# Decode attention: query parts made once and copied by ScalarE, the weights scaled on GpSimd, the first score sum behind page 5

## The chip, the cores and the metric

The kernel runs on 1 core of one Trainium2 chip. The metric is the device time of one execution in microseconds (us). The engines are named as in the profile: PE is TensorE (PEld its weight loads), DVE is VectorE, ACT is ScalarE, POOL is GpSimd, SP the sync engine that issues the DMAs. L12 is line 12 of the kernel.

## The reference, cut to what matters

One step of a two-layer decoder: an mLSTM layer and a differential-attention layer, over a prompt of 1024 tokens and over 8 sample sequences of 4 new tokens each. The change lies in the attention of the sample sequences, which read 1024 cached positions each (8 pages of 128, through a page table):

```python
def diff_mix(q, k_parts, v_parts, masks, lam):
    scores = []
    for kp, mk in zip(k_parts, masks):
        s = jnp.einsum('bqhcd,bkhcd->bhcqk', q, kp) * ATTN_SCALE
        ...
    p = jax.nn.softmax(jnp.concatenate(scores, axis=-1), axis=-1)
    w = p[:, :, 0] - lam * p[:, :, 1]
    for vp in v_parts:
        o = jnp.einsum('bhqk,bkhe->bqhe', w[..., start:start + s_len], vp)
        ...
```

There are 8 heads, two query and key parts of 64 per head, 4 queries per sequence: 64 rows of scores per sequence, each 1056 wide (1024 cached and 32 new positions). All is fp32.

## The kernel before, in words

The kernel works in phases (norm, gates, mLSTM, output projection, attention of the prompt, decode, second output projection), separated in time. The change is in `decode_phase` (L2102 to L2489). Matmuls there take each fp32 number as a high and a low part: ACT copies the data into a high part (type fp32r), DVE or POOL subtracts that from the data to get the low part, and PE multiplies both.

**Per sequence b** the decode does this. T0 to T7 (`turn`, L2418): PE transposes the eight heads of a key page in two halves of four heads, into one of three PSUM banks in turn; K0 to K7: ACT (`k_high`, L2257) copies each half into XH, DVE (`k_low`, L2336) subtracts into XL and thereby frees the bank. A half-turn has to wait for the DVE step three half-turns earlier. S0 to S3 (`score`, L2432): 16 matmuls each against two key pages, QZ holding the queries (high parts in 64 columns, low parts in the next 64). R0 to R2: ACT copies the lower 64 rows of a score bank (L2272), DVE adds the two (L2349). M: DVE adds the mask (L2355), takes the row maximum (L2356) and scales it (L2357). E: ACT takes the exponential of all 1056 columns with its sum (L2284); DVE takes the reciprocal (L2369), multiplies by a sign and lambda (L2370, giving `cf`, 64x1) and scales the 64x1056 weights with it (L2371). W: PE transposes the weights (L2452), DVE sums the two parts (L2376, L2378), ACT makes the high part (L2290, L2291), DVE the low part (L2384, L2386, both inputs in SBUF). V0 to V7 (`value`, L2457): for each value page ACT makes the high part (L2267), POOL the low part (L2240), and PE does four matmuls; then the new tokens' values (N, L2472), and ACT copies the output out (O, L2297). Q: before the keys of a sequence, ACT copies its queries' high parts from QS into QZ (L2280, two instructions) and DVE subtracts to get the low parts (L2364, two instructions with both inputs in SBUF).

**Order.** Every engine walks through a body b = 0 to 9 in an order written out by hand. In body b the keys of sequence b are turned and scored, the weights of sequence b-1 are made and its value pages 0 to 3 multiplied, and value pages 4 to 7 of sequence b-2 are finished. Bodies 2 to 7 are a hardware loop; 0 and 1 and the last two stand outside it. Body 0 has only keys, bodies 8 and 9 only weights and values.

```python
PE_ORDER = ("T0", "V4", "V5", "T1", "V6", "T2", "V7", "N", "T3", "S0", "W", "S1",
            "T4", "V0", "T5", "V1", "T6", "V2", "T7", "S2", "V3", "S3")
ACT_ORDER = ("Q", "K0", "V0", "E", "K1", "V1", "K2", "V2", "K3", "V3", "O", "W",
             "K4", "V4", "K5", "R0", "V5", "K6", "V6", "K7", "R1", "V7", "R2")
DVE_ORDER = ("Q", "K0", "K1", "E", "K2", "K3", "W", "K4", "R0", "K5", "K6", "K7", "R1", "R2", "M")
```

POOL has only the value pages' low parts, in order of pages, each behind ACT's high part. PE's V0 waits for the low weights (`wlo`, L2461), its W for the scaled weights (`wd`, L2448).

**Loads.** Key pages and value pages (512 KB each) have four slots each. SP issues them alternately, the next key page when PE has turned the page four before, the next value page when POOL has finished the page four before, all in one queue in order.

Of the kernel before, what the change touches and what calls it, by code (L numbers as in the profile page):

```python
# [17 lines left out]
ALU = mybir.AluOpType  # L18
ACT = mybir.ActivationFunctionType
F32 = mybir.dt.float32  # L20
F32R = mybir.dt.float32r
# [3 lines left out]
P = 128  # L25
D = 1024
# [77 lines left out]
def trunk_step(  # L104
# [20 lines left out]
    def phase_tensor(name, shape, dt=F32):  # L125

        return scratch[-1].enter_context(nc.sbuf_tensor(name, shape, dt))
# [27 lines left out]
    with ctx:  # L155
# [1944 lines left out]


        def decode_phase():  # L2102
            take = area(AREA - 3 * P * NT // 2 - 3 * TS)
            G = 2 * P
            NEW = PAGES * P
            ROWS = H * 2 * DS
# [1 line left out]
            VB = take(4, D)  # L2108
            SR, SX = take(TOK), take(TOK)
            AVS = take(D)  # L2110
            QS = take(H, TS)
            WS = take(NB * TS)
            sgn, mx, nm, sm, rc, cf = (take(1) for _ in range(6))
            QZ = WH[:, 0:H * 136]
            WTS = WH[:, 1088:1088 + NB * 64].rearrange("p (a c) -> p a c", a=NB)

            VH2 = phase_tensor("VH2", [P, 2, D], F32R)
            VH = [WH[:, 1664 + s * D:1664 + (s + 1) * D] for s in range(2)] + [VH2[:, s, :] for s in range(2)]
            VL = [WL[:, s * D:(s + 1) * D] for s in (0, 1, 3, 4)]
# [1 line left out]
            d_in, d_avs, d_yr = sem("d_in"), sem("d_avs"), sem("d_yr")  # L2121
            k_ld = [sem(f"d_k{s}") for s in range(4)]
            v_ld = [sem(f"d_v{s}") for s in range(4)]
            ini, pre, pre2, tp, kh, kl, sc, slo, add, mxs, exd, wd, wtp, wr, whi, wlo, vh, vl, av, avd, avc, qh, ql, vn = (
                sem(f"d_{s}") for s in ("ini", "pre", "pre2", "tp", "kh", "kl", "sc", "slo", "add", "mx", "ex", "w", "wtp",
                                        "wr", "whi", "wlo", "vh", "vl", "av", "avd", "avc", "qh", "ql", "vn"))
            dch = sem("d_dve")

            S_AT = [(BK[2], 0, G), (BK[2], G, G), (BK[3], 0, G), (BK[6], 0, G + TS)]
# [7 lines left out]

            PE_ORDER = ("T0", "V4", "V5", "T1", "V6", "T2", "V7", "N", "T3", "S0", "W", "S1",
                        "T4", "V0", "T5", "V1", "T6", "V2", "T7", "S2", "V3", "S3")
            ACT_ORDER = ("Q", "K0", "V0", "E", "K1", "V1", "K2", "V2", "K3", "V3", "O", "W",  # L2140
                         "K4", "V4", "K5", "R0", "V5", "K6", "V6", "K7", "R1", "V7", "R2")
            DVE_ORDER = ("Q", "K0", "K1", "E", "K2", "K3", "W", "K4", "R0", "K5", "K6", "K7", "R1", "R2", "M")

            def sequences(eng, body, links=None, per=0):

# [11 lines left out]
            def has_keys(b):  # L2157

                return not isinstance(b, int) or b < DB
# [17 lines left out]
            with nc.Block() as block:  # L2177
# [57 lines left out]
                @block.gpsimd  # L2235
                def _(pool):
                    with pool.Fori(0, DB) as i:
                        for p in range(PAGES):
                            pool.wait_ge(vh, PAGES * i + p + 1)
                            nc.gpsimd.tensor_tensor(VL[p % 4], VB[:, p % 4, :], VH[p % 4].bitcast(F32), ALU.subtract)\  # L2240
                              .then_inc(vl, 1)

                @block.scalar
                def _(act):
                    act.wait_ge(d_in, 48)
                    act.wait_ge(pre, 1)
                    act.activation(QS, BK[2][:, 0:H * TS].rearrange("p (h t) -> p h t", h=H), ACT.Copy)
                    act.activation(XH[:, :, NEW:TOK], BK[2][:, H * TS:2 * H * TS].rearrange("p (h t) -> p h t", h=H),
                                   ACT.Copy).then_inc(pre2, 1)
                    act.activation(VHN[0:TS, :], AVS[0:TS, :], ACT.Copy).then_inc(vn, 1)  # L2250
                    act.wait_ge(pre2, 1)
                    act.wait_ge(ini, 2)

                    def body(b):
                        i = b - 1
# [18 lines left out]
                        def queries():  # L2274

                            wait(act, sc, 4 * b)
                            for c in range(2):
                                rows = slice(DK * c, DK * c + DK)
                                dst = QZ.rearrange("p (h r) -> p h r", r=136)[rows, :, DS * c:DS * c + DS]
                                act.activation(dst, QS[rows, :, bass.ds(b * DS, DS)], ACT.Copy).then_inc(qh, 1)  # L2280

                        def exponentials():
                            act.wait_ge(mxs, i + 1)
# [34 lines left out]
                def _(dve):  # L2318
# [7 lines left out]
                    dve.wait_ge(ini, 2)  # L2326
                    dve.wait_ge(pre2, 1)
                    v.tensor_tensor(XL[:, :, NEW:TOK], BK[2][:, H * TS:2 * H * TS].rearrange("p (h t) -> p h t", h=H),
                                    XH[:, :, NEW:TOK].bitcast(F32), ALU.subtract).then_inc(vn, 1)
                    dve.wait_ge(vn, 2)  # L2330
                    v.tensor_tensor(VLN[0:TS, :], AVS[0:TS, :], VHN[0:TS, :].bitcast(F32), ALU.subtract).then_inc(vn, 1)

                    def body(b):
# [22 lines left out]
                            links.link(v.tensor_reduce(mx[0:64, :], SR[0:64, :], AX, ALU.max, negate=True))  # L2356
                            v.tensor_scalar(nm[0:64, :], mx[0:64, :], ATTN_SCALE, None, ALU.mult).then_inc(mxs, 1)  # L2357

                        def queries():
                            for c in range(2):  # L2360
                                rows = slice(DK * c, DK * c + DK)
                                z = QZ.rearrange("p (h r) -> p h r", r=136)[rows, :, :]
                                dve.wait_ge(qh, 2 * b + c + 1)
                                v.tensor_tensor(z[:, :, 64 + DS * c:64 + DS * c + DS], QS[rows, :, bass.ds(b * DS, DS)],  # L2364
                                                z[:, :, DS * c:DS * c + DS].bitcast(F32), ALU.subtract).then_inc(ql, 1)

                        def shares():
                            dve.wait_ge(exd, i + 1)
                            links.link(v.reciprocal(rc[0:64, :], sm[0:64, :]))  # L2369
                            links.link(v.tensor_tensor(cf[0:64, :], rc[0:64, :], sgn[0:64, :], ALU.mult))  # L2370
                            v.tensor_scalar(SR[0:64, :], SR[0:64, :], cf[0:64, :], None, ALU.mult).then_inc(wd, 1)  # L2371

                        def weights_low():

# [13 lines left out]

                        for step in DVE_ORDER:
                            if step[0] == "K" and has_keys(b):  # L2390
                                k_low(int(step[1]))
                            elif step[0] == "R" and has_keys(b):
                                add_rows(int(step[1]))
                            elif step == "M" and has_keys(b):
                                maximum()
                            elif step == "Q" and has_keys(b):
                                queries()
                            elif step == "E" and has_weights(b):
                                shares()
                            elif step == "W" and has_weights(b):  # L2400
                                weights_low()
                    sequences(dve, body, links, 4)

                @block.tensor
                def _(pe):
# [9 lines left out]
                    def body(b):  # L2415
# [16 lines left out]
                        def score(g):  # L2432
                            bank, at, n = S_AT[g]
                            pe.wait_ge(kl, 2 * PAGES * b + 4 * (g + 1))
                            if g == 0:
                                pe.wait_ge(ql, 2 * b + 2)

                            wait(pe, add, 3 * i + (1, 1, 2, 3)[g])
                            m = 0
                            for h in range(H):  # L2440
                                for k in (XH, XL):
                                    x = nc.tensor.matmul(bank[:, at:at + n], QZ[:, h * P:(h + 1) * P],
                                                         k[:, h, g * G:g * G + n], start=(m == 0), stop=(m == 2 * H - 1))
                                    m += 1
                            x.then_inc(sc, 1)
# [88 lines left out]
```

## Time and profile before

| what | value |
|---|---|
| median of 3 runs | 1851.96 us (1850.69 to 1852.35) |
| the profiled execution | 1853.36 us |
| its span, first to last instruction | 1851.6 us |
| decode, first body's keys to the last output | about 1449 to 1733 us of the span |
| busy share of the span | PE 91%, PEld 74%, DVE 55%, ACT 45%, POOL 23% |
| mean granted PE clock | 0.950 |
| DMA | 172 MB, mean 93 GB/s |

Times in the trace are from the start of the span. A line of a timeline has the start, the length, the engine, the source line, the operation, what it writes and reads, the count of merged instructions, and in brackets how long the engine stood idle before it and what ended that. The windows view gives the busy time of each engine in a stretch, and the clock granted to PE in it as a share of full speed.

### The profile page before, as it was taken

The numbers are of one execution on the slowest core, as the hardware profiler recorded it, in microseconds if no ns is written. First come the engines' busy times: TensorE is split into PE (matmuls) and PEld (weight loads), VectorE is DVE, ScalarE is ACT, GpSimd is POOL, SyncE is SP. The second block draws the span as 40 slices with busy tenths as digits, with TensorE's granted clock in tenths as the row PEclk, the third lists the DMA queues.
The fourth block names the chain that finished last, engine by engine and source line by source line (L and its number), as shares of the span: only waits on it lengthen the run. The fifth ranks groups of instructions, "written<-read, shape, count | busy, mean of one in ns | idle before, by whom it ended". The sixth has DMA issues, their size and how long they took to land. (4 is left out here: it accounts for less than half of the span.)

```text
span 1851.6 us, 31067 instructions
## 1 busy us (share of the span) xinstructions
PE 1680.6 (91%) x9243; PEld 1376.7 (74%) x9243; DVE 1016.0 (55%) x2648; ACT 840.2 (45%) x1994; POOL 434.5 (23%) x862
## 2 busy tenths in 40 slices
PE   5299999999999997988999999999999688887798
PEld 4288888888888876778778778778788567665576
DVE  4534444445454443354777767767766465666343
ACT  5343444344343432242555545555545456666322
POOL 1011212212122120010122221222222066566201
PEclk8599999999999997998999999999999889899799
DMA  6123050350421204322221211211101578886713
GB/s 167 27 58 72 25 94 2 92 93 1 94 43 51 38 2 143 98 85 62 62 57 41 69 47 39 64 52 46 43 12 35 201 244 277 265 272 223 256 53 112
DMA packets 164760, 172.00 MB, mean 93 GB/s; under 512 B 14634, under 2 KB 133834, under 8 KB 164658
## 3 DMA queue, kind: packets, MB, share of 16 engines
q1 hardware_dynamic: 161538, 170.78, 31.6%
q8 instruction: 45, 0.74, 0.2%
q14 instruction: 57, 0.47, 0.1%
q10 hardware_dynamic: 3120, 0.01, 0.1%
HBM read 141.85 MB, written 28.91 MB: 92 GB/s over the span
## 5 line engine op out<-in xcount | busy, mean ns | idle before, releaser
L1017 PE MATMUL PS<-WH,XH 128*128 128x512 f32 x512 | 212.4, 415 | 0.0
L1017 PE MATMUL PS<-WH,XL 128*128 128x512 f32 x512 | 201.9, 394 | 0.0
L1017 PE MATMUL PS<-WL,XH 128*128 128x512 f32 x512 | 201.9, 394 | 0.0
L1997 PE MATMUL PS<-W,XH 128*128 128x512 f32 x384 | 123.8, 403 | 0.0
L1751 ACT ACTIVATE WORK<-PD,WORK 128x896 f32<-128x896 f32 (+7 forms) x128 | 94.9, 741 | 62.8 <-DVE WORK L1918 57.8
L1017 PEld LDWEIGHTS PS<-WH,XL 128*128 128x128 f32 x512 | 96.2, 188 | 22.8
L1017 PEld LDWEIGHTS PS<-WH,XH 128*128 128x128 f32 x512 | 96.8, 189 | 19.8
L1017 PEld LDWEIGHTS PS<-WL,XH 128*128 128x128 f32 x512 | 96.8, 189 | 17.2
L1815 POOL TENSOR_SCALAR WORK<-WORK 128x1 f32<-128x1 f32 x64 | 19.9, 311 | 362.4 <-ACT WORK L1785 362.4
L2240 POOL TENSOR_TENSOR WL<-WORK,WH 128x1024 fp32r<-128x1024 f32 x32 | 75.8, 2369 | 101.4 <-ACT WH L2267 101.4
L1917 DVE TENSOR_REDUCE WORK<-PD 128x1 f32<-128x896 f32 (+7 forms) x128 | 96.4, 753 | 4.0 <-issue 1.8
L796 POOL TENSOR_SCALAR WORK<-WORK 128x1 f32<-128x1 f32 (+1 forms) x72 | 13.6, 189 | 345.3 <-ACT WORK L678 345.3
L1997 PE MATMUL PS<-WH,XH 128*128 128x512 f32 (+2 forms) x224 | 85.8, 383 | 3.1 <-ACT WH L1716 3.1
L2428 PE MATMUL PS<-cst,RAW 128*128 128x128 f32 x384 | 61.1, 299 | 29.8 <-DVE XL L2340 26.6
L844 DVE SCALAR_TENSOR_TENSOR WORK<-PS,WORK 128x128 f32<-128x128 f32 (+1 forms) x72 | 20.0, 278 | 120.9 <-PE PS L1043 119.6
L2240 POOL TENSOR_TENSOR WL<-WORK,VH 128x1024 fp32r<-128x1024 f32 x32 | 77.1, 2411 | 26.2 <-ACT VH L2267 26.2
L1997 PE MATMUL PS<-WH,XL 128*128 128x512 f32 (+2 forms) x224 | 82.2, 367 | 0.0
L1997 PE MATMUL PS<-WL,XH 128*128 128x512 f32 (+2 forms) x224 | 82.0, 366 | 0.0
L2428 PEld LDWEIGHTS PS<-cst,RAW 128*128 128x128 f32 x384 | 48.9, 154 | 41.9 <-DVE XL L2340 30.0
L2340 DVE TENSOR_TENSOR XL<-PS,XH 128x512 fp32r<-128x512 f32 x96 | 62.7, 684 | 31.3 <-ACT XH L2260 30.7
L1997 PEld LDWEIGHTS PS<-W,XH 128*128 128x128 f32 x384 | 68.8, 188 | 14.8 <-issue 1.4
L2079 PEld LDWEIGHTS PS<-RAW 128*128 128x128 f32 x576 | 73.6, 191 | 6.5 <-issue 1.4
(364 smaller groups left out, 4691.3 us busy)
## 6 DMA issues: line engine op xcount, KB each, us to landing
RAW<-in_cache_k SPq DMA_DIRECT2D x64, 512.0 KB, 4.8
WORK<-in_cache_v SPq DMA_DIRECT2D x64, 512.0 KB, 4.5
RAW<-in_w_in_a SPq DMA_DIRECT2D x40, 512.0 KB, 7.4
out<-WORK SPq DMA_DIRECT2D x16, 512.0 KB, 3.0
out<-RAW SPq DMA_DIRECT2D x16, 512.0 KB, 3.2
RAW<-in_w_in_b SPq DMA_DIRECT2D x60, 128.0 KB, 2.3
RAW<-in_w_kv SPq DMA_DIRECT2D x56, 128.0 KB, 2.2
WORK<-d_G SPq DMA_DIRECT2D x8, 528.0 KB, 12.3
```

Source lines behind the costliest of these rows:

```text
L796: links.link(g_.tensor_scalar(var[0:n, b:b + 1], ssq[0:n, b:b + 1], 4.0 / P, 16 * EPS, ALU.mult, ALU.add))
L844: v.scalar_tensor_tensor(AT[0:n, t % 2, 0:n], B_S[0:n, 0:n], K_SCALE, EX[0:n, t % 2, 0:n], ALU.mult, ALU.mult).then_inc(at, 1)
L1017: last = nc.tensor.matmul(bank, x[:, k, tok(t, P)], wkvoz(w)[:, k, :], start=(k == i == 0), stop=(k == KT - 1 and i == 2))
L1751: act.activation(PR[:, c, 0:n], S[c][:, 0:n], ACT.Exp, scale=ATTN_SCALE, bias=nm[:, c:c + 1], accum_out=sm[:, c:c + 1]).then_inc(ex, 1)
L1815: links.link(g.tensor_scalar(var[:, b:b + 1], ssq[:, b:b + 1], 1.0 / P, EPS, ALU.mult, ALU.add))
L1917: links.link(v.tensor_reduce(mx[:, c:c + 1], S[c][:, 0:n], AX, ALU.max, negate=True))
L1997: last = nc.tensor.matmul(out, x[:, k, at(NT - 1 - s)], w[:, k, cols], start=(k == i == 0), stop=(k == KT - 1 and i == 2))
L2079: x = nc.tensor.matmul(B_O, WT[:, kb, :], V[:, kb, :], start=(kb == 0), stop=(kb == t))
L2240: nc.gpsimd.tensor_tensor(VL[p % 4], VB[:, p % 4, :], VH[p % 4].bitcast(F32), ALU.subtract)\
L2340: v.tensor_tensor(XL[cols], T_BANK[2 * p + j].rearrange("p (h t) -> p h t", h=4), XH[cols].bitcast(F32), ALU.subtract).then_inc(kl, 1)
L2428: x = nc.tensor.transpose(T_BANK[u][:, h * P:(h + 1) * P], KB[:, p % 4, (4 * j + h) * P:(4 * j + h + 1) * P], ident)
```

## The change

The high and low parts of the queries of all 8 sequences are made once, ahead of the first body: ACT writes QH (instead of QS) and DVE one subtraction, QL. In each body ACT copies four small pieces, two of QH and two of QL, into QZ; DVE has no query step any more. This query step stands behind K1 in ACT's order instead of ahead of K0. DVE's E step ends with `cf`; the multiplication of the 64x1056 weights with it is a GpSimd instruction with a broadcast operand, in POOL's queue between value pages 1 and 2. In DVE's order R0 stands behind K5 instead of ahead of it. Semaphores `qh` and `ql` give way to `qz` (four counts per body) and `cfd`; a body has three links in DVE's own chain instead of four.

```diff
         def decode_phase():
-            take = area(AREA - 3 * P * NT // 2 - 3 * TS)
+            take = area(AREA - 3 * P * NT // 2 - 11 * TS)
...
-            QS = take(H, TS)
...
+            QH = WH[:, 1664 + 3 * D:1664 + 3 * D + H * TS].rearrange("p (h t) -> p h t", h=H)
+            QL = phase_tensor("QL", [P, H, TS], F32R)[:, :, :]
...
-            ACT_ORDER = ("Q", "K0", "V0", "E", "K1", "V1", "K2", "V2", "K3", "V3", "O", "W",
+            ACT_ORDER = ("K0", "V0", "E", "K1", "Q", "V1", "K2", "V2", "K3", "V3", "O", "W",
                          "K4", "V4", "K5", "R0", "V5", "K6", "V6", "K7", "R1", "V7", "R2")
-            DVE_ORDER = ("Q", "K0", "K1", "E", "K2", "K3", "W", "K4", "R0", "K5", "K6", "K7", "R1", "R2", "M")
+            DVE_ORDER = ("K0", "K1", "E", "K2", "K3", "W", "K4", "K5", "R0", "K6", "K7", "R1", "R2", "M")
...
                 def _(pool):
                     with pool.Fori(0, DB) as i:
                         for p in range(PAGES):
+                            if p == 2:
+                                pool.wait_ge(cfd, i + 1)
+                                nc.gpsimd.tensor_tensor(SR[0:64, :], SR[0:64, :], cf[0:64, :].to_broadcast([64, TOK]), ALU.mult)\
+                                  .then_inc(wd, 1)
                             pool.wait_ge(vh, PAGES * i + p + 1)
...
                 def _(act):
                     act.wait_ge(d_in, 48)
                     act.wait_ge(pre, 1)
-                    act.activation(QS, BK[2][:, 0:H * TS].rearrange("p (h t) -> p h t", h=H), ACT.Copy)
+                    act.activation(QH, BK[2][:, 0:H * TS].rearrange("p (h t) -> p h t", h=H), ACT.Copy)
...
                     act.wait_ge(ini, 2)
+                    act.wait_ge(vn, 2)
...
                         def queries():
 
                             wait(act, sc, 4 * b)
-                            for c in range(2):
-                                rows = slice(DK * c, DK * c + DK)
-                                dst = QZ.rearrange("p (h r) -> p h r", r=136)[rows, :, DS * c:DS * c + DS]
-                                act.activation(dst, QS[rows, :, bass.ds(b * DS, DS)], ACT.Copy).then_inc(qh, 1)
+                            for part, q in ((0, QH), (64, QL)):
+                                for c in range(2):
+                                    rows = slice(DK * c, DK * c + DK)
+                                    at = part + DS * c
+                                    act.activation(QZ.rearrange("p (h r) -> p h r", r=136)[rows, :, at:at + DS],
+                                                   q[rows, :, bass.ds(b * DS, DS)].bitcast(F32), ACT.Copy).then_inc(qz, 1)
...
                     dve.wait_ge(pre2, 1)
                     v.tensor_tensor(XL[:, :, NEW:TOK], BK[2][:, H * TS:2 * H * TS].rearrange("p (h t) -> p h t", h=H),
-                                    XH[:, :, NEW:TOK].bitcast(F32), ALU.subtract).then_inc(vn, 1)
+                                    XH[:, :, NEW:TOK].bitcast(F32), ALU.subtract)
+                    v.tensor_tensor(QL, BK[2][:, 0:H * TS].rearrange("p (h t) -> p h t", h=H), QH.bitcast(F32), ALU.subtract)\
+                     .then_inc(vn, 1)
...
-                        def queries():
-                            for c in range(2):
-                                rows = slice(DK * c, DK * c + DK)
-                                z = QZ.rearrange("p (h r) -> p h r", r=136)[rows, :, :]
-                                dve.wait_ge(qh, 2 * b + c + 1)
-                                v.tensor_tensor(z[:, :, 64 + DS * c:64 + DS * c + DS], QS[rows, :, bass.ds(b * DS, DS)],
-                                                z[:, :, DS * c:DS * c + DS].bitcast(F32), ALU.subtract).then_inc(ql, 1)
-
                         def shares():
                             dve.wait_ge(exd, i + 1)
                             links.link(v.reciprocal(rc[0:64, :], sm[0:64, :]))
-                            links.link(v.tensor_tensor(cf[0:64, :], rc[0:64, :], sgn[0:64, :], ALU.mult))
-                            v.tensor_scalar(SR[0:64, :], SR[0:64, :], cf[0:64, :], None, ALU.mult).then_inc(wd, 1)
+                            v.tensor_tensor(cf[0:64, :], rc[0:64, :], sgn[0:64, :], ALU.mult).then_inc(cfd, 1)
...
                             if g == 0:
-                                pe.wait_ge(ql, 2 * b + 2)
+                                pe.wait_ge(qz, 4 * b + 4)
```

## Rows read from the trace of the kernel before

**Rows 1.** Windows, one per decode body: stretch, length, busy time of each engine, granted clock.

```profile
1508.72:1541.25 32.53, 27.38 (x175) 22.05 (x174) 20.61 (x31) 21.17 (x35) 19.06 (x9) 0.90 0.79 252
1541.25:1572.84 31.59, 26.31 (x175) 21.36 (x174) 20.28 (x31) 21.18 (x35) 19.05 (x9) 0.95 0.84 273
...
sum 223.20, PE 183.68 PEld 149.23 DVE 140.22 ACT 146.94 POOL 132.47; mean PE 26.24 PEld 21.32 DVE 20.03 ACT 20.99 POOL 18.92
```

**Rows 2.** Timeline of PE in the body from 1541.05: start, length, what, idle before.

```profile
1541.05 1.04 PE L2428 MATMUL PS<-cst,RAW 128*128 128x128 f32 x8
...
1547.81 0.90 PE L2428 MATMUL PS<-cst,RAW 128*128 128x128 f32 x4 [3.45 <-DVE XL L2340]
1548.37 0.78 PE L2465 MATMUL PD<-VH,WH 128*64 128x512 f32 x1
...
1551.64 0.47 PE L2465 MATMUL PD<-VH,WH 128*64 128x512 f32 x1
...
1554.64 0.36 PE L2442 MATMUL PS<-XH,WH 128*128 128x256 f32 x1
...
1556.70 0.71 PE L2452 MATMUL PD<-cst,WORK 64*128 64x64 f32 x8
...
1560.17 0.48 PE L2465 MATMUL PD<-WH 128*64 128x512 f32 x1
...
1565.39 0.66 PE L2428 MATMUL PD<-cst,RAW 128*128 128x128 f32 x4 [1.83 <-DVE XL L2340]
...
1567.60 0.36 PE L2442 MATMUL PS<-XH,WH 128*128 128x256 f32 x1
```

**Rows 3.** Timeline of DVE in the same body.

```profile
1543.98 0.15 DVE L2357 TENSOR_SCALAR WORK<-WORK 64x1 f32<-64x1 f32 x1
1544.65 2.39 DVE L2364 TENSOR_TENSOR WH<-WORK,WH 64x32 fp32r<-64x32 f32 x2 [0.52 <-issue]
1547.07 1.29 DVE L2340 TENSOR_TENSOR XL<-PS,XH 128x512 fp32r<-128x512 f32 x2
...
1550.36 2.96 DVE L2371 TENSOR_SCALAR WORK<-WORK 64x1056 f32<-64x1056 f32 x1
...
1558.92 0.43 DVE L2384 TENSOR_TENSOR WH<-WORK,WH 128x256 fp32r<-128x256 f32 x1 [0.60 <-ACT WH L2291]
```

**Rows 4.** Timeline of POOL in the same body.

```profile
1544.43 2.34 POOL L2240 TENSOR_TENSOR WL<-WORK,WH 128x1024 fp32r<-128x1024 f32 x1 [1.81 <-ACT WH L2267]
1550.37 2.38 POOL L2240 TENSOR_TENSOR WL<-WORK,WH 128x1024 fp32r<-128x1024 f32 x1 [3.61 <-ACT WH L2267]
```

**Rows 5.** Timeline of ACT in the same body.

```profile
1541.67 0.48 ACT L2280 ACTIVATE WH<-WORK 64x32 fp32r x2
...
1548.75 0.60 ACT L2260 ACTIVATE XH<-PS 128x512 fp32r<-128x512 f32 x1 [2.76 <-PE PS L2428]
...
1561.38 1.06 ACT L2267 ACTIVATE WH<-WORK 128x1024 fp32r<-128x1024 f32 x1 [0.27 <-PE PD L2465]
...
1564.99 0.60 ACT L2260 ACTIVATE XH<-PS 128x512 fp32r<-128x512 f32 x1
```

**Rows 6.** Timeline of DVE behind the last keys.

```profile
1704.68 0.76 DVE L2371 TENSOR_SCALAR WORK<-WORK 64x1056 f32<-64x1056 f32 x1
...
1708.66 1.59 DVE L2384 TENSOR_TENSOR WH<-WORK,WH 128x256 fp32r<-128x256 f32 x1 [1.48 <-ACT WH L2291]
1710.16 2.32 DVE L2386 TENSOR_TENSOR WH<-WORK,WH 32x32 fp32r<-32x32 f32 x1
```

**Rows 7.** Timeline of POOL and of PE in that stretch.

```profile
1707.62 4.82 POOL L2240 TENSOR_TENSOR WL<-WORK,VH 128x1024 fp32r<-128x1024 f32 x2
...
1712.58 0.66 PE L2465 MATMUL PD<-WH 128*64 128x512 f32 x1 [6.26 <-DVE WH L2386]
```

**Rows 8.** POOL groups by form: shapes, count, busy, mean ns.

```profile
L780 POOL TENSOR_TENSOR WORK<-WORK,COL 128x128 f32<-128x128 f32 x64 | 25.6, 400 | 174.1 <-ACT WORK L760 174.1
```

**Rows 9.** Tile RAW, key pages and weights: time of a DMA to landing.

```profile
DMA to landing us min/median/max: 3.5/4.8/6.9
```

More of the change, by code:

```diff
@@ L2123, in decode_phase @@
             v_ld = [sem(f"d_v{s}") for s in range(4)]
-            ini, pre, pre2, tp, kh, kl, sc, slo, add, mxs, exd, wd, wtp, wr, whi, wlo, vh, vl, av, avd, avc, qh, ql, vn = (
+            ini, pre, pre2, tp, kh, kl, sc, slo, add, mxs, exd, wd, wtp, wr, whi, wlo, vh, vl, av, avd, avc, qz, cfd, vn = (
                 sem(f"d_{s}") for s in ("ini", "pre", "pre2", "tp", "kh", "kl", "sc", "slo", "add", "mx", "ex", "w", "wtp",
-                                        "wr", "whi", "wlo", "vh", "vl", "av", "avd", "avc", "qh", "ql", "vn"))
+                                        "wr", "whi", "wlo", "vh", "vl", "av", "avd", "avc", "qz", "cf", "vn"))
             dch = sem("d_dve")
@@ L2395, in body @@
                                 maximum()
-                            elif step == "Q" and has_keys(b):
-                                queries()
                             elif step == "E" and has_weights(b):
@@ L2401, in body @@
                                 weights_low()
-                    sequences(dve, body, links, 4)
+                    sequences(dve, body, links, 3)
                 @block.tensor
```

## The prediction

> **What bounds the kernel now.** I read the profile's page first for where the decode lies, then the windows, one per decode body, then the timeline of PE in one body with the idle time ahead of each step, then DVE, POOL and ACT in the same body. The seven bodies with keys take 223.20 us, 31.89 each; most take 31.6, some 32.5 with a lower granted clock [rows 1]. No engine is busy for a whole body (PE 26.2, ACT 21.0, DVE 20.0, POOL 18.9 on the mean), so the length is set by waits. PE's timeline shows two: 3.45 us ahead of the second half of T1 and 1.83 us ahead of the second half of T6, both released by DVE's low part of the keys [rows 2]. All positions below are us after T0 of the body that starts at 1541.05.
>
> Why DVE is late for T1 is read from its own timeline [rows 3]: M ends at 3.08, the loop's turn takes 0.52, and then the two query subtractions L2364, of 64x32 each, take 2.39. They end 0.3 us after POOL's value page, which runs from 1544.43 to 1546.77 [rows 4]: DVE was held while POOL ran. K0 starts only at 6.02, and T1's second half 0.74 behind it, at 6.76. The same holds for the weights' scaling L2371: 2.96 us beside POOL's page of 2.38 us [rows 3, 4], 0.76 us where it started ahead of the page [rows 6].
>
> PE also loses by its clock. From T1's second half to V7 it takes 3.83 us, from T6's second half to S2, the same steps (half a turn, one value page, a whole turn), 2.21 us [rows 2]. After the 3.45 us of idling the matmuls are at the lower level (0.78 against 0.47 us), after the 1.83 us they are not. The spell costs 1.62 us.
>
> **The change part by part. Queries.** DVE's K0 follows the loop's turn directly, at 3.60, and T1's second half at 4.34 instead of 6.76; the wait shrinks from 3.45 to 1.03. I take the clock to stay up, as it did behind 1.83. Then S0 comes at 4.34 + 6.83 - 1.62 = 9.55 and PE is ready for W 2.06 later, at 11.6 (15.65 before) [rows 2]. ACT's query step costs 0.48 for two pieces [rows 5], so 0.96 for four. It no longer delays K0 but lies between K1 and V1, where the value pages wait behind it (next part). The one new subtraction QL stands beside ACT's copy of the new values and costs nothing; without that cover it is one instruction like K0's half, 0.65 us, once.
>
> **The multiplication on POOL.** No row shows one of 64x1056. A multiplication with a broadcast operand of 128x128 takes 0.40 [rows 8], a subtraction of 128x1024 takes 2.38 [rows 4]; the line through both gives 0.40 + 928 x 1.98 / 896 = 2.45. Bounds: 1.2 if half the partitions took half the time, 4.9 if the broadcast were read as a second slow stream. I take 2.45, since the row nearest in kind is no slower than the line. Its start hangs on page 1: ACT gets T1's second half 0.94 behind its start (at the low clock, [rows 2, 5]; I take 0.7), copies it by 5.6, then Q to 6.6 and V1 (1.06, as V4 in [rows 5]) to 7.7; POOL does page 1 until about 10.1 and the multiplication until 12.6. So W starts at 12.6: a new wait of 1.0 on PE, with S1, T4 and V0 behind it. DVE loses its 2.96, but PE had no wait behind that, so this alone gives nothing.
>
> The Trainium skill speaks against this step: "GPSIMD Engine Reference", section 4.1 (Engine selection), wants elementwise work on VectorE and gives GpSimd about twice its time for two inputs. With the 0.76 that DVE needs unhindered and twice that on GpSimd, 8 sequences would lose 6 us if the step lay on the path; the rows of the loop show 2.96 on DVE.
>
> **The low weights.** L2384 comes 2.22 behind W's start [rows 2, 3], at 14.8. POOL then does page 2 (12.6 to 15.0) and page 3 (to 17.4) with no gap, as ACT has both ready by about 12. What two DVE instructions do against two such pages stands behind the last keys: L2384 took 1.59 instead of 0.43, L2386, of 32x32 only, 2.32, until POOL's pair was done, and V0 started right then, at 1712.58 [rows 3, 6, 7]. So the low weights are there at 17.45, not at 15.4 (14.8 and some 0.6 for the two), and V0 starts at 17.6 instead of 19.12; PE, ready 3.47 behind W at 16.1, waits 1.5. Gain up to here: 1.5.
>
> **R0 behind K5.** V4 on ACT starts 1.21 behind V0 and takes 1.06 [rows 2, 5], K5's half on ACT 0.6, on DVE 0.7: T6's second half comes at 3.6 behind V0 instead of 5.22. But ACT gets to K6 4.82 behind V0 as before [rows 5], since its own order from V4 to K6 is unchanged. K6's half then takes 0.6 on ACT and 0.75 on DVE, so T7's second half can't start before 6.2, where PE would be there at 5.4 (3.6 + 2.21 less half a turn of 0.4): of 1.6 us half comes back as a wait on K6. S2 lies at 6.6 (half a turn later) instead of 7.43 behind V0: gain 0.8. From S2 on nothing is moved.
>
> **The sum.** One body: 31.59 - 1.5 - 0.8 = 29.3; against the mean, with the longer spells of low clock gone, 31.89 - 29.3 = 2.6. I take 2.5 for each of the six bodies 2 to 7: 15.0. Body 1 has no pages 4 to 7 in front, and V0 there too hangs on POOL's page 3: 2.0 (0 to 3.5). Body 0 gains about 1.3 at T6 and loses the 0.96 of Q between K1 and K2: 0.4. Behind the last keys V0 waits for POOL's pages 2 and 3 as before [rows 7], and the multiplication now stands ahead of them: a loss of 2.4. In all 15.0 + 2.0 + 0.4 - 2.4 = 15.0. The profiled execution took 1853.36 us on a span of 1851.6, so 1838.4; it lies 1.4 us above the median of the runs, so the median would be near 1837. I give 1838.
>
> **What is costed at nothing.** DMA: its share is 0.84 and would be 0.91 in 29.3 us [rows 1]. SP's queue runs in order, and key page 7 goes out behind value page 6, so behind POOL's page 2, at about 16.2; T7 needs it at 22.5, 6.3 us later, against 4.8 to landing on the median and 6.9 at most [rows 9]. If it were late, up to 0.6 us a body. POOL would be busy for 21.5 of 29.3 us, ACT for 21.5: neither becomes the bound.
>
> **The rivals.**
>
> *The low weights slip through.* L2384 is ready 0.2 us ahead of the end of POOL's page 2; if both low-weight steps got in ahead of page 3, V0 would start at 16.1 and a body would take 27.8: 6 x 4.1 + 2.4 - 0.4 = 26.6 less, 1827 us. Against it speaks [rows 6], where the second step was held through the whole next page. Chance 0.17.
>
> *The clock stays low.* PE would now wait four times, 0.8 to 1.5 us each. The granted clock was 0.90 and not 0.95 in a body with a longer spell [rows 1]. If each body still had one spell of 1.62, 9.7 of the 15.0 would be lost: 1848 us. Chance 0.15.
>
> *The multiplication takes over the path.* It stands on POOL ahead of pages 2 and 3, whose end releases V0. From a length of 4.8 us on (V0 at 19.9) a body is no shorter than before. At the upper bound of 4.9 the six bodies gain 6 x 0.1, body 1 loses 0.5 and the end 4.9: 1853.4 + 4.8 = 1858, slower. For it speaks no row, against it [rows 8]. Engine selection in the Trainium skill, named above, points the same way. Chance 0.07.
>
> *Nothing comes of it:* the waits only move from T1 and T6 to W, V0 and T7, and make up the whole difference (a body of 31.5 or more). All three new waits are in the sum above with 3.3 us together. Chance 0.04.
>
> **How the numbers follow.** Forecast 0.57, and the rivals 0.17, 0.15, 0.07 and 0.04. A difference under 0.2% (3.7 us) can't be told from none. Forecast, slipping weights and low clock are all faster: 0.89; same 0.04; slower 0.07. The range runs from 1825, just below the slipping weights, to 1848, the low clock, and leaves out the last two cases and half of the low clock's. The forecast's own range, with 0.7 us a body for the key page and for the start of page 1, is 1833 to 1843.
>
> **What would show it.** Right: L2364 gone, K0 about 0.5 us behind M; T1's second half idle about 1 us ahead of it, with 0.47 us matmuls behind it; a multiplication of about 2.45 us on POOL, W released by it; L2386 held to the end of page 3 and V0 behind it; T6's wait under 0.5, a wait of about 0.8 at T7; bodies of 29.3. Wrong: a multiplication far from 2.45, matmuls of 0.63 us behind T1, waits on key pages, or V0 at 16.

## The result, and the profile after

| | before | after |
|---|---|---|
| median | 1852.15 us (1850.69 to 1853.47, 4 runs) | 1829.14 us (1828.26 to 1830.63, 4 runs) |
| ratio, 95% interval | | 0.9877 (0.986 to 0.9894) |
| the profiled execution, its span | 1853.36, 1851.6 us | 1828.26, 1826.0 us |
| granted PE clock | 0.950 | 0.961 |

The kernel became 23.0 us faster; 1838 was forecast, with 1825 to 1848 as the range. One body is taken from ACT's copy out of S3's bank (64x288) to the next one. The two profiled spans differ by 25.6 us: 2.54 lie ahead of the end of body 0, 3.44 in body 1 (31.63 to 28.19), 20.03 in bodies 2 to 7, and behind the last keys 0.64 go the other way, until the output projection's first transposes (33.16 to 33.80); the last phase differs by 0.23. The 2.54 hold the earlier phases, which no edit touches, and can't be split; the rest is 22.8 us and agrees with the medians.

Windows of the kernel after, body 4 and the sum over bodies 2 to 7 (six; [rows 1] has seven):

```profile
1559.80:1588.37 28.57, 25.38 (x175) 20.05 (x174) 17.07 (x28) 21.20 (x38) 20.86 (x10) 1.00 0.90 308
...
sum 171.34, PE 151.26 PEld 120.64 DVE 102.60 ACT 127.03 POOL 125.20; mean PE 25.21 PEld 20.11 DVE 17.10 ACT 21.17 POOL 20.87
```

All six last 28.49 to 28.59 us, and the granted clock is 1.00 in every one, where [rows 1] shows 0.90 and 0.95. Timeline of PE in body 4, which begins at 1559.60 and answers to [rows 2]; positions below are from there:

```profile
1559.60 1.03 PE L2427 MATMUL PS<-cst,RAW 128*128 128x128 f32 x8
...
1563.79 0.66 PE L2427 MATMUL PS<-cst,RAW 128*128 128x128 f32 x4 [0.87 <-DVE XL L2350]
1564.20 0.47 PE L2464 MATMUL PD<-VH,WH 128*64 128x512 f32 x1
...
1569.00 0.36 PE L2441 MATMUL PS<-XH,WH 128*128 128x256 f32 x1
...
1571.65 0.69 PE L2451 MATMUL PD<-cst,WORK 64*128 64x64 f32 x8 [0.53 <-POOL WORK L2242]
...
1576.54 0.42 PE L2464 MATMUL PD<-WH 128*64 128x512 f32 x1 [1.20 <-POOL WL L2245]
...
1580.03 0.65 PE L2427 MATMUL PD<-cst,RAW 128*128 128x128 f32 x4
...
1581.78 0.65 PE L2427 MATMUL PS<-cst,RAW 128*128 128x128 f32 x4 [0.17 <-DMA RAW<-in_cache_k]
...
1582.71 0.65 PE L2427 MATMUL PS<-cst,RAW 128*128 128x128 f32 x4 [0.27 <-DVE XL L2350]
1583.12 0.36 PE L2441 MATMUL PS<-XH,WH 128*128 128x256 f32 x1
...
1588.17 1.03 PE L2427 MATMUL PS<-cst,RAW 128*128 128x128 f32 x8
```

T1's second half waits 0.87 and not 3.45, and the value matmuls behind it take 0.47 and not 0.78. T7 waits 0.17 for its key page and then 0.27 for DVE in this body; in the other five no key page is waited for, and T7's second half waits 0.66 or 0.67. W now waits 0.53, for GpSimd's multiplication, and V0 1.20; the wait put down to POOL there is that for the low weights, as DVE shows.

```profile
1562.53 0.15 DVE L2367 TENSOR_SCALAR WORK<-WORK 64x1 f32<-64x1 f32 x1
1563.04 1.29 DVE L2350 TENSOR_TENSOR XL<-PS,XH 128x512 fp32r<-128x512 f32 x2 [0.36 <-issue]
...
1565.90 0.15 DVE L2372 TENSOR_TENSOR WORK<-WORK 64x1 f32<-64x1 f32 x1
...
1573.84 2.50 DVE L2385 TENSOR_TENSOR WH<-WORK,WH 128x256 fp32r<-128x256 f32 x1 [0.60 <-ACT WH L2299]
1576.27 0.17 DVE L2387 TENSOR_TENSOR WH<-WORK,WH 32x32 fp32r<-32x32 f32 x1
```

The query step L2364 of [rows 3] is gone: K0 comes 0.36 behind M. L2372 makes the factor at 6.45. L2385, the low weights, 0.43 long in [rows 3], takes 2.50, and L2387 goes through in 0.17 behind it. POOL, which answers to [rows 4]:

```profile
1567.11 2.39 POOL L2245 TENSOR_TENSOR WL<-WORK,WH 128x1024 fp32r<-128x1024 f32 x1 [2.00 <-ACT WH L2273]
1569.47 1.94 POOL L2242 TENSOR_TENSOR WORK<-WORK 64x1056 f32<-64x1056 f32 x1
1571.37 4.69 POOL L2245 TENSOR_TENSOR WL<-WORK,VH 128x1024 fp32r<-128x1024 f32 x2
```

The multiplication (L2242) takes 1.94 and follows page 1 without a gap. Pages 2 and 3 run from 11.77 to 16.46; page 3 starts about 1573.72, L2385 is ready at 1573.84, and it ends 0.28 behind page 3. The timeline merges the two pages; the start of page 3 is taken from page 2's length, 2.35. ACT's query step, which answers to [rows 5], stands ahead of page 1's high part:

```profile
1564.97 0.47 ACT L2287 ACTIVATE WH<-WH 64x32 fp32r x2
1565.46 0.48 ACT L2287 ACTIVATE WH<-QL 64x32 fp32r x2
1565.97 1.06 ACT L2273 ACTIVATE WH<-WORK 128x1024 fp32r<-128x1024 f32 x1
```

DVE and then PE behind the last keys, which answer to [rows 6, 7]:

```profile
1686.31 2.10 DVE L2385 TENSOR_TENSOR WH<-WORK,WH 128x256 fp32r<-128x256 f32 x1 [0.60 <-ACT WH L2299]
1688.33 0.17 DVE L2387 TENSOR_TENSOR WH<-WORK,WH 32x32 fp32r<-32x32 f32 x1
```

```profile
1683.67 1.08 PE L2451 MATMUL PD<-cst,WORK 64*128 64x64 f32 x8 [4.86 <-POOL WORK L2242]
...
1688.61 0.66 PE L2464 MATMUL PD<-WH 128*64 128x512 f32 x1 [3.75 <-POOL WL L2245]
```

W waits 4.86 for the multiplication and V0 then 3.75; before, V0 waited 6.26 and W 0.76.

### The profile page after: what moved, and what is told of

It is laid out like the page before. It is cut to its first block and busy times, and to the rows that moved or that the text cites. A ratio compares the mean times of both kernels' runs of the same rounds, so it can differ in the third digit from the quotient of the medians.

```text
span 1826.0 us, 31059 instructions
## 1 busy us (share of the span) xinstructions
PE 1665.9 (91%) x9243; PEld 1363.5 (75%) x9243; DVE 992.9 (54%) x2625; ACT 841.0 (46%) x2010; POOL 447.8 (25%) x870
## 5 line engine op out<-in xcount | busy, mean ns | idle before, releaser
L1017 PEld LDWEIGHTS PS<-WH,XL 128*128 128x128 f32 x512 | 96.2, 188 | 22.8
L760 ACT ACTIVATE WORK<-PS 128x512 f32<-128x512 f32 x64 | 38.3, 598 | 90.4 <-PE PS L1017 90.4
L2079 PE MATMUL PS<-RAW 128*128 128x128 f32 x576 | 75.0, 275 | 1.3 <-DVE WORK L1884 1.3
```

Source lines behind the costliest of these rows:

```text
L760: act.activation(PJS[:, t % 2, :, 0:2 * P], PJ[(3 + t) % 2].rearrange("p (a c) -> p a c", a=2), ACT.Copy).then_inc(ev, 1)
L1017: last = nc.tensor.matmul(bank, x[:, k, tok(t, P)], wkvoz(w)[:, k, :], start=(k == i == 0), stop=(k == KT - 1 and i == 2))
L2079: x = nc.tensor.matmul(B_O, WT[:, kb, :], V[:, kb, :], start=(kb == 0), stop=(kb == t))
```

## The experiments

Bodies are from each run's own trace, since the place where the decode begins varies between executions of one kernel (see e11).

| run | what | median us | ratio (95%) | body 1 | mean of 2 to 7 |
|---|---|---|---|---|---|
| before | | 1851.6 to 1852.7 | 1 | 31.63 | 31.89 |
| e2 | R0 alone | 1842.74 | 0.995 (0.9934 to 0.9967) | 31.76 | 30.78 |
| e4 | POOL's multiplication alone | 1844.03 | 0.9958 (0.9944 to 0.9972) | 28.48 | 31.86 |
| e11 | e4 again | 1847.66 | 0.9972 (0.9954 to 0.9989) | 28.47 | 31.86 |
| e3 | query part alone | 1824.74 | 0.9859 (0.9842 to 0.9875) | 28.82 | 27.51 |
| e1 | query part and R0 | 1815.9 | 0.9811 (0.979 to 0.9832) | 26.36 | 26.70 |
| after, e12 | all three | 1829.14, 1830.38 | 0.9877, 0.9881 (0.9864 to 0.9897) | 28.19, 28.22 | 28.56, 28.56 |
| e5 | after, second operand a full tile | 1836.39 | 0.9911 (0.9895 to 0.9928) | 28.73 | 29.06 |
| e7 | after, low weights ahead of page 3 | 1819.76 | 0.9825 (0.9809 to 0.9842) | 26.89 | 27.14 |
| e8 | after, multiplication ahead of page 1 | 1822.25 | 0.9839 (0.9823 to 0.9856) | 27.32 | 27.58 |
| e9 | e1, e7's wait and K6 ahead of R0 | 1813.51 | 0.9793 (0.9777 to 0.9809) | 25.84 | 26.89 |
| e10 | e1 and e7's wait | 1813.96 | 0.9789 (0.9773 to 0.9805) | 25.94 | 26.56 |

**e1: the multiplication back on DVE.**

```diff
-                            if p == 2:
-                                pool.wait_ge(cfd, i + 1)
-                                nc.gpsimd.tensor_tensor(SR[0:64, :], SR[0:64, :], cf[0:64, :].to_broadcast([64, TOK]), ALU.mult)\
-                                  .then_inc(wd, 1)
...
+                            v.tensor_scalar(SR[0:64, :], SR[0:64, :], cf[0:64, :], None, ALU.mult).then_inc(wd, 1)
```

> The changed kernel with one part undone: the weights are scaled by DVE again, behind its K1, as before the change. Theory (POOL's queue): in the changed kernel V0 is released by the end of POOL's value page 3, and the multiplication of 1.94 us stands ahead of pages 2 and 3. DVE has its factor 6.45 us after T0, when POOL is between page 0 (ends at 5.5) and page 1 (starts at 7.5), so the multiplication is not held on DVE (0.76 us); page 3 ends 1.9 us earlier, W needs no wait, V0 starts at 15.0 instead of 16.9: bodies of 26.6 us instead of 28.6, the end 2 us shorter too, 1814 us. Rival (DVE freed): the gain of the change came from taking 2.96 us off DVE; then DVE is held again, L2350 of K2 is late by some 2 us, and the time is 1835 to 1850 us.

1815.9 us: the change without its GpSimd part is 13.2 us faster than the change, 1.86 a body. DVE and POOL in a steady body (T0 at 1555.60):

```profile
1562.09 0.76 DVE L2369 TENSOR_SCALAR WORK<-WORK 64x1056 f32<-64x1056 f32 x1
...
1569.27 1.21 DVE L2382 TENSOR_TENSOR WH<-WORK,WH 128x256 fp32r<-128x256 f32 x1 [0.60 <-ACT WH L2295]
```

```profile
1558.73 2.38 POOL L2241 TENSOR_TENSOR WL<-WORK,WH 128x1024 fp32r<-128x1024 f32 x1 [1.56 <-ACT WH L2269]
1563.11 2.38 POOL L2241 TENSOR_TENSOR WL<-WORK,WH 128x1024 fp32r<-128x1024 f32 x1 [1.99 <-ACT WH L2269]
1565.46 4.74 POOL L2241 TENSOR_TENSOR WL<-WORK,VH 128x1024 fp32r<-128x1024 f32 x2
```

DVE reaches the scaling 6.5 behind T0, in POOL's gap between pages 0 and 1 (1561.11 to 1563.11), and does it in 0.76. In the kernel before it got there while page 1 ran and took 2.96 [rows 3, 4]; it was the removed query step that made it late. The low weights (L2382) are ready at 13.67 and still held until page 3 ends at 14.60, but PE is not: W and V0 don't wait, and V0 comes at 15.08 instead of 16.94.

**e2 and e3: R0 alone, and the query part alone.** e2 is the kernel before with this line; e3 is e1 with it undone.

```diff
-            DVE_ORDER = ("Q", "K0", "K1", "E", "K2", "K3", "W", "K4", "R0", "K5", "K6", "K7", "R1", "R2", "M")
+            DVE_ORDER = ("Q", "K0", "K1", "E", "K2", "K3", "W", "K4", "K5", "R0", "K6", "K7", "R1", "R2", "M")
```

> The kernel before, with R0 behind K5 in DVE's order and nothing else. Theory: of the 1.83 us ahead of T6's second half nearly all goes, and half of it comes back ahead of T7's second half, which waits for ACT to reach K6 behind R0 and V5: 0.85 us a body, 1 us in body 0, about 1845 us. Rival: nothing comes back, 1.8 us a body, 1838 us. Third: DVE's R0 late makes a new wait and nothing is gained, 1852 us.

> The kernel before, with the query part alone (QH and QL made once, four copies on ACT behind K1): weights scaled on DVE, R0 ahead of K5. Theory: the wait ahead of T1's second half falls from 3.4 to 0.9 us, the matmuls behind it run at 0.47 us, the scaling on DVE is not held since it falls between POOL's pages 0 and 1; bodies of 27.5 us, 1821 us. Rival (DVE freed): the scaling is held for 2.9 us and takes back most: bodies of 30 us, 1840 us.

PE's waits in a steady body of e2, then of e3, and DVE's scaling in e3:

```profile
1560.99 0.66 PE L2428 MATMUL PS<-cst,RAW 128*128 128x128 f32 x4 [0.66 <-DVE XL L2340]
...
1573.20 0.66 PE L2428 MATMUL PS<-cst,RAW 128*128 128x128 f32 x4 [3.43 <-DVE XL L2340]
```

```profile
1536.68 0.66 PE L2424 MATMUL PS<-cst,RAW 128*128 128x128 f32 x4 [0.90 <-DVE XL L2346]
...
1552.78 0.66 PE L2424 MATMUL PD<-cst,RAW 128*128 128x128 f32 x4 [1.83 <-DVE XL L2346]
```

```profile
1566.51 0.76 DVE L2369 TENSOR_SCALAR WORK<-WORK 64x1056 f32<-64x1056 f32 x1
```

In e2 the 1.83 ahead of T6's second half has become 0.66 at T7's, and the 3.43 at T1 stays: 1.11 a body, where 0.85 was expected, and 1842.74 us for 1845. In e3 the 3.45 has become 0.90, the scaling takes 0.76 on DVE and the 1.83 stays: bodies of 27.51 for 27.5 expected and 1824.74 us for 1821. That is 4.38 a body, more than the whole change gives. Adding R0 to e3 (that is e1) gives 0.81 more, the 0.8 of the prediction.

**e4: the multiplication on POOL alone**, in the kernel before.

```diff
+                            if p == 2:
+                                pool.wait_ge(cfd, i + 1)
+                                nc.gpsimd.tensor_tensor(SR[0:64, :], SR[0:64, :], cf[0:64, :].to_broadcast([64, TOK]), ALU.mult)\
+                                  .then_inc(wd, 1)
...
-                            v.tensor_scalar(SR[0:64, :], SR[0:64, :], cf[0:64, :], None, ALU.mult).then_inc(wd, 1)
```

> The kernel before, with the weights' scaling on POOL between value pages 1 and 2 and nothing else. Theory: DVE's step of 2.96 us had no wait of PE behind it and POOL's page 3 then ends about 18.5 us after T0, still ahead of V0 at 19.1: bodies unchanged at 31.6, the end up to 2 us longer, 1850 to 1855 us. Rival (DVE freed): 2 to 3 us a body less, 1832 to 1838 us.

A miss by the time: 7.6 us faster on the medians, where nothing or a small loss was expected. In its trace the steady bodies are as expected (31.86 against 31.89); body 1 is not. There DVE's scaling of the kernel before, held by POOL's page (1483.34 to 1485.69), stands ahead of the low parts that T3's second half waits for; DVE, then PE, of the kernel before, body 1:

```profile
1483.44 2.81 DVE L2371 TENSOR_SCALAR WORK<-WORK 64x1056 f32<-64x1056 f32 x1
```

```profile
1486.91 1.12 PE L2428 MATMUL PS<-cst,RAW 128*128 128x128 f32 x4 [2.98 <-DVE XL L2340]
1487.68 0.56 PE L2442 MATMUL PS<-XH,WH 128*128 128x256 f32 x1
```

The same place in e4:

```profile
1482.03 0.66 PE L2431 MATMUL PS<-cst,RAW 128*128 128x128 f32 x4 [0.59 <-DVE XL L2344]
1482.45 0.36 PE L2445 MATMUL PS<-XH,WH 128*128 128x256 f32 x1
```

The wait of 2.98 is 0.59, and the score matmul behind it is at 0.36 and not 0.56: 3.15 us in this one body. The query part alone wins 2.81 there too: in e3 the scaling starts before the page and takes 0.76. In the traces the end gives 0.81 back (33.97 against 33.16, with V0 2.06 later). So some 2.3 us of the edit are seen, and e11 asked where the rest is from.

**e11: e4 without any edit.**

> The kernel of e4_pool_only once more, without any edit. Its profiled execution was its slowest (1848.12 against a median of 1844.03 us), so its trace doesn't show where 7.6 us on the median went. Theory (the multiplication on GpSimd helps in body 1 alone, where it takes 2.8 us of held scaling away from ahead of DVE's part of page 3, and the rest is earlier phases): in a new trace body 1 is 28.5 us and the steady bodies are on the mean 31.5 to 32.0 again, median 1844 to 1848 us. Rival (it helps in the steady bodies too, by fewer stretches of low clock): steady bodies of 31.2 or less on the mean.

Body 1 is 28.47 and the steady ones are 31.86 again, as the theory has it. But this profiled execution too was the slowest of its run, 1854.36 us, 6.24 above that of e4, and body 0 ends 6.23 later (1480.83 and 1474.60): the whole difference between the two traces lies ahead of the bodies compared here.

So the question stays open for the executions near 1844 us. Seven of the eleven of e4 and e11 took 1843.4 to 1846.6 us, at a mean granted clock of 0.957 to 0.959; the four others, the two traced ones among them, took 1848.1 us or more at 0.949 to 0.953. The 24 executions of the kernel before that ran beside the experiments took 1849.95 to 1856.12 us, all at 0.948 to 0.953. Most executions with this edit thus had a higher clock than any without it. Whether that is in the steady bodies (the rival) or elsewhere is not shown, since none of them has a trace.

**e5: the multiplication with a full second operand** (so with other numbers than the factor).

```diff
-                                nc.gpsimd.tensor_tensor(SR[0:64, :], SR[0:64, :], cf[0:64, :].to_broadcast([64, TOK]), ALU.mult)\
+                                nc.gpsimd.tensor_tensor(SR[0:64, :], SR[0:64, :], SX[0:64, :], ALU.mult)\
```

> The changed kernel, with the second operand of GpSimd's multiplication read as a full 64x1056 tile instead of a broadcast column; so the weights are multiplied with other numbers. It asks why that instruction took 1.94 us and not the 2.45 of the prediction. Theory (the broadcast is what makes it short, a second stream costs as in the value pages): 2.35 to 2.5 us, W, pages 2 and 3 and V0 0.45 later, a body 29.0 instead of 28.57, 1829 + 8 x 0.45 = 1832.7 us. Rival (the 64 rows instead of 128 make it short, the kind of operand does nothing): 1.94 us again and 1829 us, within 1.5.

POOL's group of the multiplication (eight: busy us, mean ns), after and then e5:

```profile
L2242 POOL TENSOR_TENSOR WORK<-WORK 64x1056 f32<-64x1056 f32 x8 | 15.5, 1939 | 0.0
```

```profile
L2242 POOL TENSOR_TENSOR WORK<-WORK 64x1056 f32<-64x1056 f32 x8 | 19.5, 2444 | 0.0
```

2444 ns, the 2.45 of the prediction, for two streams; the broadcast column saves 0.5. A body is 0.50 longer, just that much, so the instruction's length lies fully on the path. The median is 7.3 us up. In the traces bodies 1 to 7 make 3.6 us (0.54 and 6 x 0.51), and V0 behind the last keys comes 0.48 later; so the expected 3.6 us are there, and what makes the medians differ by more is not shown.

**e7: the low weights ahead of page 3.**

```diff
+                            if p == 3:
+                                pool.wait_ge(wlo, i + 1)
                             pool.wait_ge(vh, PAGES * i + p + 1)
```

> The changed kernel, with GpSimd made to wait for DVE's low weights ahead of value page 3, so that these find GpSimd idle. It asks whether V0 comes late because the low weights are held until page 3 is done. Theory (they are held): the first low-weight step takes 0.43 us instead of 2.50, V0 comes when PE is ready for it, 15.7 us after T0 instead of 16.94, and the idle 1.20 ahead of V0 goes; page 3 ends 0.8 later, which costs nothing as V3 is multiplied 9 us later. Seven bodies by 1.2 and 2.0 behind the last keys: 1829 - 10.4 = 1818.6 us. Rival (the step is slow by itself, or what it reads is late): it stays near 2.5 us, V0 no earlier, page 3 late, 1829 us or some more.

DVE, POOL and PE's V0 in a steady body (T0 at 1560.66):

```profile
1574.88 0.42 DVE L2387 TENSOR_TENSOR WH<-WORK,WH 128x256 fp32r<-128x256 f32 x1 [0.60 <-ACT WH L2301]
1575.22 0.17 DVE L2389 TENSOR_TENSOR WH<-WORK,WH 32x32 fp32r<-32x32 f32 x1
```

```profile
1572.42 2.37 POOL L2247 TENSOR_TENSOR WL<-WORK,VH 128x1024 fp32r<-128x1024 f32 x1
1575.56 2.39 POOL L2247 TENSOR_TENSOR WL<-WORK,VH 128x1024 fp32r<-128x1024 f32 x1 [0.76 <-DVE WH L2389]
```

```profile
1576.14 0.48 PE L2466 MATMUL PD<-WH 128*64 128x512 f32 x1
```

0.42 instead of 2.50: the step is short when POOL is idle. V0 comes at 15.48 without a wait, the bodies lose 1.42 each, and the time 9.4 us for 10.4 expected. A wait added to POOL made the kernel faster.

**e8: the multiplication ahead of page 1.**

```diff
-                            if p == 2:
+                            if p == 1:
                                 pool.wait_ge(cfd, i + 1)
```

> The changed kernel, with the multiplication one page further ahead in GpSimd's queue, between value pages 0 and 1, where GpSimd idles for 2.0 us. It asks whether the cost of the multiplication on GpSimd is its own length or its place. Theory (place): the factor is there 6.45 us after T0, the multiplication runs to 8.4, page 1 starts 0.9 later than before and page 3 ends at 15.5 instead of 16.46; W waits no more, V0 comes at 15.8 to 16.0, a body is 27.6, and the time 1829 - 8 x 1.0 = 1821 us; that is still slower than the 1815.9 us with the multiplication on DVE. Rival (any place on GpSimd costs the same, since page 1 is pushed back): 1829 us, within 2.

POOL, and PE's V0, in a steady body (T0 at 1558.44):

```profile
1564.96 1.94 POOL L2242 TENSOR_TENSOR WORK<-WORK 64x1056 f32<-64x1056 f32 x1 [1.00 <-DVE WORK L2372]
1566.86 2.38 POOL L2245 TENSOR_TENSOR WL<-WORK,WH 128x1024 fp32r<-128x1024 f32 x1
1569.21 4.71 POOL L2245 TENSOR_TENSOR WL<-WORK,VH 128x1024 fp32r<-128x1024 f32 x2
```

```profile
1574.40 0.42 PE L2464 MATMUL PD<-WH 128*64 128x512 f32 x1 [0.81 <-POOL WL L2245]
```

The multiplication waits 1.00 for its factor, page 3 ends at 15.48, W waits no more, and V0, at 15.96, still waits 0.81 for the held low weights: 0.98 a body, as expected. Place counts for about half of the 1.86 that GpSimd costs.

**e9 and e10: towards a better version.** Both have the multiplication on DVE and e7's wait; e9 also this:

```diff
-                         "K4", "V4", "K5", "R0", "V5", "K6", "V6", "K7", "R1", "V7", "R2")
-            DVE_ORDER = ("K0", "K1", "E", "K2", "K3", "W", "K4", "K5", "R0", "K6", "K7", "R1", "R2", "M")
+                         "K4", "V4", "K5", "K6", "R0", "V5", "V6", "K7", "R1", "V7", "R2")
+            DVE_ORDER = ("K0", "K1", "E", "K2", "K3", "W", "K4", "K5", "K6", "R0", "K7", "R1", "R2", "M")
```

> A version that could beat both kernels: the changed kernel with the multiplication on DVE again, GpSimd waiting for the low weights ahead of value page 3, and K6 ahead of R0 in the orders of both ACT and DVE. Theory: with the multiplication on DVE PE waits for nothing ahead of V0 in the steady bodies, so GpSimd's wait gives there nothing and only about 2 us behind the last keys; K6 ahead of R0 takes away the wait of 0.36 ahead of T7's second half, 6 x 0.35 = 2.1. 1815.9 - 4.1 = 1812 us. Rival (K6 does not wait for the order, and R0 pushed back makes K7 late instead): 1814 to 1818 us.

> The multiplication on DVE as in e1_scale_on_dve and GpSimd's wait for the low weights ahead of value page 3 as in e7_low_weights_first; the orders of ACT and DVE as in the changed kernel, so K6 behind R0. Theory (putting K6 ahead of R0 in e9_best cost 0.2 us a body, and all that run gained was behind the last keys): steady bodies of 26.7 us as in e1_scale_on_dve, the wait ahead of V0 behind the last keys 4.1 and not 6.3 us, 1815.9 - 2.2 = 1813.7 us by the one, 1813.5 - 1.2 = 1812.3 by the other: 1813 us. Rival (K6 ahead of R0 did help): bodies of 27 us and 1815 to 1816 us.

V0 behind the last keys, in e1 and in e10:

```profile
1675.17 0.66 PE L2461 MATMUL PD<-WH 128*64 128x512 f32 x1 [6.26 <-DVE WH L2384]
```

```profile
1671.62 0.66 PE L2463 MATMUL PD<-WH 128*64 128x512 f32 x1 [4.11 <-DVE WH L2386]
```

e7's wait takes 2.15 off there, as expected. K6 ahead of R0 gives nothing: PE's waits in a steady body of e9 are

```profile
1557.06 0.66 PE L2426 MATMUL PS<-cst,RAW 128*128 128x128 f32 x4 [1.17 <-DVE XL L2348]
...
1573.29 1.09 PE L2426 MATMUL PS<-cst,RAW 128*128 128x128 f32 x8 [0.37 <-DMA RAW<-in_cache_k]
```

against 0.87 at T1 and 0.39 at T7's second half in e10; the latter is gone, but T1's grew by 0.3 and T7 now waits 0.37 for its key page. The bodies of e9 are 0.33 longer than those of e10. The two medians, 1813.51 and 1813.96, can't be told apart (e9's profiled decode began earlier: body 0 ended at 1473.23, against 1475.96). Both are over 38 us below the kernel before and some 15 below the change; e10 is the version to keep, as it has the shorter bodies.

**e12: the changed kernel beside e10 and e11.**

> The changed kernel itself beside the two others, so that they stand against it on one chip. Theory and rival alike: 1829 us within 2, steady bodies of 28.5 us; if it comes out by over 3 us elsewhere, the differences between runs of different calls are worth less than taken here.

1830.38 us, 1.2 above the first time, bodies of 28.56 again. What differs is the stretch behind the last keys, here first of the first trace, then of e12:

```profile
1674.08:1707.88 33.80, 17.15 (x65) 8.55 (x64) 5.52 (x10) 12.37 (x17) 21.98 (x10) 0.83 0.65 231
```

```profile
1673.50:1708.98 35.48, 19.37 (x66) 9.12 (x64) 5.51 (x10) 12.38 (x17) 21.99 (x10) 0.71 0.63 219
```

V0 comes 14.53 us into the stretch in both. Behind it, from the middle of value page 6 on, PE's matmuls take 0.63 us in e12 and 0.39 or 0.40 in the first trace. So the same kernel differs by 1.7 us here, and a smaller difference between two traces in this stretch shows nothing by itself.

## Why the prediction was right, and where it was off

**Right in sign, range and mechanism.** The steps came at or near their places. In body 4, from T0 (forecast in brackets): K0 3.44 (3.60), T1's second half 4.19 (4.34), S0 9.40 (9.55), W 12.05 (12.6), V0 16.94 (17.6); from V0: T6's second half 3.49 (3.6), T7's wait 0.27 and 0.66 in the other five bodies (0.8), S2 6.58 (6.6). Body: 28.57 (29.3). The rivals fell: the low weights did not slip through (L2385 was held through page 3, 2.50; the prediction had the second step, L2387, held instead, to the same end), the clock did not stay low (1.00 in all six bodies), the multiplication was 1.94 and not 4.9. Of the signs of being wrong two came in part: that length, a fifth below 2.45, and the wait of 0.17 on a key page in one body.

By its number alone the result would have misled: 1829 lies outside the forecast's own range, 1833 to 1843, and next to the 1827 of the slipping weights. Only the trace tells the two apart.

**Off by 8 us (15.0 in the sum, 23.0 measured), in four terms.**
- The multiplication was sized 2.45 and took 1.94. The line was drawn through value pages with two streams; e5 shows that 2.45 is right for those, and that the broadcast makes the difference. With page 1 done 0.2 earlier than forecast this is the 0.66 of V0.
- The prediction took 2.5 a body, below its own 2.6. The mean gain was 3.34 (20.03 / 6). Of the 0.84 between them 0.66 are those of V0, 0.1 the rounding down; the two bodies of 32.5 were counted already, in the 31.89. Over six bodies this and the first point make 5.0 of the 8 us.
- Body 1 was put at 2.0 by analogy and gave 3.44. The step "PE had no wait behind that, so this alone gives nothing", right in the steady bodies of e4's traces (31.86), fails in body 1, where the held scaling stood ahead of T3 and cost 3.15. 1.4 of the 8 us.
- Behind the last keys 2.4 of loss were forecast. V0 did come 2.04 later than before, but from V0 to the output projection's first transposes it is 19.27 instead of 20.67, at a granted clock of 0.86 instead of 0.75; together 0.64, and 1.8 of the 8 us. This term is luck of one execution: in e12, with the same V0 and a clock of 0.66 behind it, the loss is 2.32 where 2.4 was forecast. Of the 0.4 in body 0 the traces show nothing sure.

**What the prediction did not ask: what the multiplication would cost on DVE in the new order.** It compared POOL's 2.45 with the 2.96 of the kernel before. Without the query step DVE gets there in POOL's gap and needs 0.76 (e1), so that 2.96 was a price of the old order alone. The query part is worth 4.38 a body, R0 0.81, and the move to POOL takes 1.86 back, in this order; put into the kernel before alone, R0 gives 1.11 and the move 0.03. Of the 1.86, e7 wins 1.42 back by the low weights alone: the move costs mostly by where it puts pages 2 and 3. W starts when the multiplication ends, and so does page 2; the low weights are ready 2.47 later and page 2 takes 2.35, so they always meet page 3 just begun.

The row-based sum thus missed a loss that a page names: the Trainium skill, "GPSIMD Engine Reference", section 4.1 (Engine selection), gives elementwise work to VectorE. The runs agree in the direction, with 1.94 against 0.76, which is 2.6 times and not two; the estimate of 6 us made from it stands against 13.2 measured, as it counts the instruction and not what stands behind it in the queue.

## What to carry to other kernels

Before a step is moved to another engine because it is slow, ask whether it is slow by itself or by what it meets; if another part of the same change removes the meeting, price the step without it (0.76, not 2.96). On a queue in order the place of an instruction can cost as much as its length: look at what the instructions behind it will collide with, and consider adding a wait (e7) so that a short instruction on the path goes ahead of a long one that nobody waits for.

## What the runs showed of the hardware

- A DVE subtraction with both inputs in SBUF that became ready 0.1 us after a GpSimd page had begun took 2.50 us, until the page's end; with GpSimd idle the same one took 0.42 (e7). The 64x1056 scaling took 0.76 with GpSimd idle (e1, e3) and 2.96 beside a page [rows 3, 4]. The Trainium skill, "SBUF — State Buffer", section "Who interferes with whom", says that two-input instructions of DVE contend with GpSimd's reads, and that the one that issues first decides; the low weights agree, held when the page had begun 0.1 us earlier. For the scaling, whose factor is only 64x1, [rows 3, 4] can't tell who was first: it and the page begin within 0.01 us of each other.
- GpSimd's 64x1056 multiplication took 1.94 us with a broadcast 64x1 operand and 2.44 with a full one (e5).
- One kernel ended body 0 of its decode 6.2 us apart in two executions (e4, e11) with bodies 1 to 7 equal within 0.1; another took 33.80 and 35.48 us behind the last keys (after, e12), at a granted clock of 0.83 and 0.71. Parts of a decode are better compared body by body than by the total.
